# Recurrent scores as 64x64 chunk products, moved into the state update, with the second group's solve one step behind

## What is computed

```python
def _rwkv7_scan(r, w, k, v, kk, a):
    def step(state, inp):
        r_t, w_t, k_t, v_t, kk_t, a_t = inp
        sa = jnp.einsum('bhij,bhj->bhi', state, -kk_t)
        state = (state * w_t[:, :, None, :]
                 + sa[..., None] * (kk_t * a_t)[:, :, None, :]
                 + v_t[..., None] * k_t[:, :, None, :])
        y = jnp.einsum('bhij,bhj->bhi', state, r_t)
        return state, y
```

## Time and profile before

| | |
|---|---|
| median of 3 runs | 3903.39 us (3902.7 to 3903.99) |
| profiled execution | 3901.91 us, its span 3900.1 us |
| PE / PEld busy | 91% / 74% |
| DVE / ACT / POOL busy | 34% / 31% / 33% |
| mean granted TensorE clock | 0.943 |
| recurrent stage, four tiles | from 2056 to 2331 us of the span |

### The profile page before, as it was taken

How to read it: one execution, slowest core, us unless ns; L and a number is a source line. 1 busy time by engine, 2 the same in 40 slices (tenths; PEclk the granted TensorE clock), 3 DMA queues, 4 the chain that set the end, 5 groups by cost and what they waited for, 6 DMA issues and landing times. The chain is left out here.

```text
span 3900.1 us, 39057 instructions
## 1 busy us (share of the span) xinstructions
PE 3554.1 (91%) x16504; PEld 2867.9 (74%) x16504; DVE 1344.4 (34%) x1893; ACT 1213.1 (31%) x1795; POOL 1293.6 (33%) x531
## 2 busy tenths in 40 slices
PE   7868999999999999998977889999988989989987
PEld 6766778877677788875766767788876758767866
DVE  5963331232333312124463334201165143032432
ACT  4323332232443322334332112322243522242232
POOL 3423244443152444421420003344423404414432
PEclk9979999999999999989988889899989999999998
DMA  3212122222131222221220012222222202202231
GB/s 138 87 49 81 60 92 97 98 95 81 34 119 59 93 97 97 96 74 43 84 92 33 1 45 94 71 97 97 92 81 81 92 22 92 92 30 84 92 108 60
DMA packets 82807, 305.30 MB, mean 78 GB/s; under 512 B 8997, under 2 KB 10825, under 8 KB 81354
## 3 DMA queue, kind: packets, MB, share of 16 engines
q1 hardware_dynamic: 78368, 280.61, 21.3%
q10 hardware_dynamic: 4266, 22.21, 1.5%
HBM read 291.77 MB, written 11.02 MB: 78 GB/s over the span
## 5 line engine op out<-in xcount | busy, mean ns | idle before, releaser
L2569 POOL TENSOR_TENSOR WL<-RW,WH 128x1024 fp32r<-128x1024 f32 x527 | 1293.4, 2457 | 2574.1 <-ACT WH L261 2573.9
L266 PE MATMUL PS<-XH,WH 128*128 128x512 f32 x2968 | 1178.3, 397 | 100.3 <-POOL WL L2569 40.7
L267 PE MATMUL PS<-XL,WH 128*128 128x512 f32 x2968 | 1167.9, 394 | 0.0
L268 PE MATMUL PS<-XH,WL 128*128 128x512 f32 x2968 | 1166.8, 393 | 0.0
L261 ACT ACTIVATE WH<-RW 128x1024 fp32r<-128x1024 f32 x527 | 552.7, 1052 | 807.1 <-PE PS L268 661.3
L266 PEld LDWEIGHTS PS<-XH,WH 128*128 128x128 f32 x2968 | 565.2, 190 | 241.5 <-issue 57.5
L268 PEld LDWEIGHTS PS<-XH,WL 128*128 128x128 f32 x2968 | 564.9, 190 | 119.6
L267 PEld LDWEIGHTS PS<-XL,WH 128*128 128x128 f32 x2968 | 565.3, 190 | 117.8 <-issue 2.4
L266 PE MATMUL PS<-YH,WH 128*128 128x512 f32 (+1 forms) x928 | 351.9, 379 | 30.9 <-DVE YL L831 9.7
L267 PE MATMUL PS<-YL,WH 128*128 128x512 f32 (+1 forms) x928 | 350.1, 377 | 0.0
L268 PE MATMUL PS<-YH,WL 128*128 128x512 f32 (+1 forms) x928 | 349.9, 377 | 0.0
(11 more groups left out here) (449 smaller groups left out, 3363.3 us busy)
## 6 DMA issues: line engine op xcount, KB each, us to landing
RW<-in_units SPq DMA_DIRECT2D x527, 512.0 KB, 3.2
spill<-X ACTq DMA_DIRECT2D x2, 2048.0 KB, 7.7
X<-spill ACTq DMA_DIRECT2D x2, 2048.0 KB, 8.0
X<-in_xT SPq DMA_DIRECT2D x8, 256.0 KB, 7.1
A<-spill ACTq DMA_DIRECT2D x1, 2048.0 KB, 10.2
out_T<-X ACTq DMA_DIRECT2D x1, 2048.0 KB, 7.4
spill<-X ACTq DMA_DIRECT2D x1, 1536.0 KB, 5.1
spill_gates<-X ACTq DMA_DIRECT2D x1, 1536.0 KB, 6.1
```

Source lines behind the costliest of these rows:

```text
L266: mm(out, hi, xh, start=first, stop=False)
L267: mm(out, hi, xl, start=False, stop=False)
L268: return mm(out, lo, xh, start=False, stop=last)
L2569: nc.gpsimd.tensor_tensor(WL[:, u % SPLIT, :], RW[:, u % RAW, :], WH[:, u % SPLIT, :].bitcast(F32), ALU.subtract).then_inc(split_done, 1)
```

## The change

- The score products are cut by chunk. Instead of full 128-token products, each head makes two 64x64 results per matrix, one for each chunk, with 64 rows and 64 columns of the array: the off-diagonal chunk blocks are no longer computed. Six products per pair of heads become twelve, with 64, 128 and 128 columns in place of 128, 256 and 256. Their results lie in banks 4g to 4g + 3, so the groups no longer share banks.
- The masks are applied to the diagonal blocks alone: twelve instructions of 64 partitions x 256 elements in place of six of 128 x 512. The zeros elsewhere are written once at t = 0 by eight memsets (six of 128x512, one of 128x1024, one of 128x2048) that follow the wait for the DMAs. The wait for the previous tile's `y.mm` stands before the last four masks instead of before the first.
- The products `.w` become a function of their own, `weights_pe`.
- `scores_pe` of the next tile's group 0 is issued inside `state_pe`, between `u.mm` and `s.mm` of the first chunk; it waits for the previous `.at` of group 0. Group 1's scores come after the state and wait for `y` and `st`.
- The solve of group 0 starts after its own `.w`; `.w` and `.rhs` of group 1 come after group 0's step 0, and group 1's step s - 1 follows group 0's step s. Only the first application waits for `.rhs`.

```diff
-        scores = PS[:, 0:7:6, 0:256].rearrange("p w (j c) -> p w j c", j=2)
+        halves = [slice(0, 64), slice(64, P)]
         def scores_pe(st, t, g):
+            i, B = f"r{t}.{g}", 4 * g
+            if t:
+                st.wait(*([f"y{t - 1}", f"st{2 * t - 1}"] if g else [f"r{t - 1}.0.at"]))
+            for q in range(2):
+                j = 2 * g + q
+                for c in range(2):
+                    tok = slice(t * P + 64 * c, t * P + 64 * c + 64)
+                    for w, b in enumerate(halves):
+                        mm(PS[halves[c], B + w, q * 64:(q + 1) * 64], AR[j][b, t, 0, halves[c]], T(j)[b, tok], start=True, stop=True)
...
+            for q in range(2):
+                last = nc.tensor.transpose(PS[:, B + 2, 256 + q * P:256 + (q + 1) * P], AR[2 * g + q][:, t, 0, :], ident)
+            st.do(last, i + ".scores")
+        def weights_pe(st, t, g):
...
             st.wait(i + ".masked")
...
         def scores_dve(st, t, g):
+            if t == 0 and g == 0:
+                st.wait("ma.out1", "gb.out", "rk.out")
+                for x in (GS[0][0], GS[0][1], GS[0][2], GS[1][0], GS[1][1], GS[1][2]):
+                    st.do(v.memset(x, 0.0))
+                st.do(v.memset(RHS[:, :, P:2 * P], 0.0))
+                st.do(v.memset(RB, 0.0))
             st.wait(i + ".scores")
...
+            for c, r in enumerate(halves):
+                masked(q4(G2)[r, :, :, halves[c]], k[c][:, :, :, 0, :], "strictT", c)
+                masked(q4(G0)[r, :, :, halves[c]], a[c], "sub16", c)
+                masked(q4(G1)[r, :, :, halves[c]], b[c][:, :, :, 0, :], "sub16T", c)
+                masked(R4[r, :, :, P + 64 * c:P + 64 * c + 64], a[c], "off16", c)
+            if t:
                 st.wait_ge(*reached(f"y.mm{t - 1}"))
+            for c, r in enumerate(halves):
+                masked(RB0[r, :, :, halves[c]], b[c][:, :, :, 1, :], "chunkT", c)
+                masked(RB1[r, :, :, halves[c]], k[c][:, :, :, 1, :], "chunkT", c, i + ".masked")
...
             if step == 0:
                 product(0, lambda n: blk(G1, n), lambda n: blk(G0, n), ".d2")
                 product(1, lambda n: blk(G0, n), lambda n: blk(G1, n), ".d2t")
+                st.wait(i + ".rhs")
                 apply(G1, ".a1")
...
                 st.do(last, f"u.mm{n}")
+                if cc == 0 and t < TT - 1:
+                    scores_pe(st, t + 1, 0)
...
         def rw_pe(pe, st, e):
+            scores_pe(st, 0, 0)
             for t in range(TT):
-                scores_pe(st, t, 0)
                 scores_pe(st, t, 1)
-                st.wait_ge(*reached(f"r{t}.1.rhs"))
-                for step in range(STEPS):
-                    for g in range(2):
-                        solve_pe(st, t, g, step)
+                weights_pe(st, t, 0)
+                for step in range(STEPS + 1):
+                    if step < STEPS:
+                        solve_pe(st, t, 0, step)
+                    if step == 0:
+                        weights_pe(st, t, 1)
+                    else:
+                        solve_pe(st, t, 1, step - 1)
                 state_pe(st, t)
```

More of the change, by code:

```diff
@@ L1882, in program @@
         mq = lambda name: cst(name).rearrange("p (a b c) -> p a b c", a=1, b=1).to_broadcast([P, 2, 2, P])
-        scores = PS[:, 0:7:6, 0:256].rearrange("p w (j c) -> p w j c", j=2)
+        halves = [slice(0, 64), slice(64, P)]
         def scores_pe(st, t, g):
-            i = f"r{t}.{g}"
[L1887 to L1905, removed]
@@ new lines, in scores_pe @@
+            i, B = f"r{t}.{g}", 4 * g
+            if t:
+                st.wait(*([f"y{t - 1}", f"st{2 * t - 1}"] if g else [f"r{t - 1}.0.at"]))
+            st.wait_ge(*reached("p1.turned11"))
+            for q in range(2):
[4 more added lines that the diff above has]
+                        mm(PS[halves[c], B + w, q * 64:(q + 1) * 64], AR[j][b, t, 0, halves[c]], T(j)[b, tok], start=True, stop=True)
+                for c in range(2):
+                    tok = slice(t * P + 64 * c, t * P + 64 * c + 64)
+                    for w, b in enumerate(halves):
+                        o = PS[halves[c], B + w, 128 + q * P:128 + (q + 1) * P].rearrange("p (v c) -> p v c", v=2)
+                        mm(o, T(j)[b, tok], AR[j][b, t, :, halves[c]], start=True, stop=True)
+                for c in range(2):
+                    tok = slice(t * P + 64 * c, t * P + 64 * c + 64)
+                    for w, b in enumerate(halves):
+                        o = PS[halves[c], B + 2 + w, q * P:(q + 1) * P].rearrange("p (v c) -> p v c", v=2)
+                        mm(o, T(30 + j)[b, tok], AR[j][b, t, :, halves[c]], start=True, stop=True)
@@ L1906, in scores_pe @@
+            for q in range(2):
+                last = nc.tensor.transpose(PS[:, B + 2, 256 + q * P:256 + (q + 1) * P], AR[2 * g + q][:, t, 0, :], ident)
+            st.do(last, i + ".scores")
+        def weights_pe(st, t, g):
+            i = f"r{t}.{g}"
             st.wait(i + ".masked")
-            for n, h in enumerate(heads):
+            for n, h in enumerate(heads_of(g)):
                 j, b = h // 2, 64 * (h % 2)
-                last = mm(PS[:, 5, n * 64:(n + 1) * 64], blk(G2, n), T(8 + j)[:, t * P + b:t * P + b + 64], start=True, stop=True)
+                last = mm(PS[:, 4 * g + 3, 256 + n * 64:256 + (n + 1) * 64], blk(GS[g][2], n), T(8 + j)[:, t * P + b:t * P + b + 64], start=True, stop=True)
@@ L1910, in scores_pe @@
             st.do(last, i + ".w")
         def scores_act(st, t, g):
-            i = f"r{t}.{g}"
+            i, B = f"r{t}.{g}", 4 * g
             R4 = quad(RHS, g)
             st.wait(i + ".masked", i + ".w")
-            st.do(a_.activation(R4[:, :, :, 0:64], PS[:, 5, 256:512].rearrange("p (j w c) -> p w j c", j=2, w=2), ACT.Copy))
-            st.do(a_.activation(R4[:, :, :, 64:P], q4(PS[:, 5, 0:256]), ACT.Copy), i + ".rhs")
+            if t:
+                st.wait(f"u{2 * t - 1}")
+            st.do(a_.activation(R4[:, :, :, 0:64], PS[:, B + 2, 256:512].rearrange("p (j w c) -> p w j c", j=2, w=2), ACT.Copy))
@@ L1920, in scores_dve @@
+            st.do(a_.activation(R4[:, :, :, 64:P], q4(PS[:, B + 3, 256:512]), ACT.Copy), i + ".rhs")
         def scores_dve(st, t, g):
-            i = f"r{t}.{g}"
+            i, B = f"r{t}.{g}", 4 * g
             G0, G1, G2, G3 = GS[g]
-            st.wait(i + ".scores")
-            if g == 0 and t:
-                st.wait_ge(*reached(f"y.mm{t - 1}"))
[L1926 to L1936, removed]
+            if t == 0 and g == 0:
[4 more added lines that the diff above has]
+                st.do(v.memset(RB, 0.0))
@@ new lines, in scores_dve, with masked @@
+            st.wait(i + ".scores")
+            st.settle()
+            R4, RB0, RB1 = quad(RHS, g), quad(RB[:, :, 0, :], g), quad(RB[:, :, 1, :], g)
+            def masked(out, x, name, c, done=None):
+                m = cst(name)[halves[c], halves[c]].rearrange("p (a b c) -> p a b c", a=1, b=1).to_broadcast([64, 2, 2, 64])
+                st.do(v.tensor_tensor(out, x, m, ALU.mult), done)
+            a = [PS[r, B:B + 2, 0:P].rearrange("p w (q c) -> p w q c", q=2) for r in halves]
+            b = [PS[r, B:B + 2, P:3 * P].rearrange("p w (q v c) -> p w q v c", q=2, v=2) for r in halves]
@@ new lines, in scores_dve @@
+            k = [PS[r, B + 2:B + 4, 0:2 * P].rearrange("p w (q v c) -> p w q v c", q=2, v=2) for r in halves]
+            for c, r in enumerate(halves):
[3 more added lines that the diff above has]
+                masked(R4[r, :, :, P + 64 * c:P + 64 * c + 64], a[c], "off16", c)
+            if t:
+                st.wait_ge(*reached(f"y.mm{t - 1}"))
@@ L2099, in rw_act @@
                 scores_act(st, t, 0)
[L2100 to L2103, removed]
+                for step in range(STEPS + 1):
+                    if step < STEPS:
+                        solve_act(st, t, 0, step)
+                    if step == 0:
+                        scores_act(st, t, 1)
+                    else:
+                        solve_act(st, t, 1, step - 1)
                 if t == TT - 1:
@@ L2115, in rw_dve @@
                 scores_dve(st, t, 1)
-                for step in range(STEPS):
-                    for g in range(2):
-                        solve_dve(st, t, g, step)
+                for step in range(STEPS + 1):
+                    if step < STEPS:
+                        solve_dve(st, t, 0, step)
+                    if step:
+                        solve_dve(st, t, 1, step - 1)
                 state_dve(st, t)
```

## The result

The changed kernel takes 3845.4 us (3845.0 to 3848.2) against 3903.2; the ratio is 0.985 (95% interval 0.984 to 0.987). That is 57.8 us less where 51.2 were forecast, inside the range. The profiled execution has a span of 3843.2 us, 56.9 less than before.

A forecast was written before the change was run, and what follows sets the result against it. PE's single chain in the four recurrent tiles was taken as the bound, idle before each solve. Transitions 53.0, less 4.2 for scores in the state, plus 2.4 in tile 0: 51.2 us off, 3852.2; range 3837 to 3865.

The forecast's parts named there:

- Scores of group 1: After the output copy: 48 instructions 29 ns apart, 1.4 us, plus change-over 0.33 and transposes 0.44, ending at R + 2.85.
- R: Bookmark: start of a tile's output copy, 2126.77 in tile 0 before the change.
- The two-quarter rival: Array quarters run only in pairs: 0.75 us more for six groups of scores on the path, 3856.7; chance 0.15.
- Masks: DVE's twelve half-size masks per group start 0.33 us apart, 4.1 us (5.0 at 0.42); group 1's end at R + 7.0.
- Solve: Step 0 to U: 32.5 us at full clock, plus 1.2 for the skew and 1.0 for group 1's `.w`, 34.7.
- U: Bookmark: start of a tile's first state product, 2182.34 in tile 1 before the change; forecast at R + 38.5.
- The transitions: Three stretches from R to the next U: 17.1 us shorter in tile 1, 17.95 in tiles 2 and 3, 53.0 together.
- Scores inside the state update: First product needing DVE's addition comes 2.9 us after U instead of 1.47: 1.4 us later, three times, 4.2 lost.
- Tile 0: Memsets delay the masks by 6.5 us, yet the solve starts at 2075.8 instead of 2080.89: 2.4 us won, bounds 1.4 to 4.
- S: Bookmark: DVE's first instruction after the spill has landed, 2063.10 before; forecast the same.
- The clock in the state update: Low granted clock over state and outputs, 3.4 us lost per tile; change left at nought, 13.6 us if it never fell.
- The rival of a clock that never falls: The clock never falls in the recurrent stage: 3838.6 us; chance 0.13.

The follow-up runs named there:

- the run of halves in turn: Changed kernel with the same 64x64 score products, but one column half of the array finished before the other; 3854.9 us.
- the run without it: Changed kernel without the skew: group 1's `.w` stays behind group 0's step 0, then the groups go in step; 3844.4 us.
- the quarters in the old order: Changed kernel's 64x64 score products, twelve masks and memsets, with the three walks of the kernel before; 3906.2 us, ratio to before 1.001.
- the run with scores in both chunks: Changed kernel with group 0's scores divided: first pair of heads in chunk 0 of the state update, second pair and transposes in chunk 1; 3845.5 us.
- the scores after the state update: Changed kernel with group 0's scores of the next tile issued after the state update instead of inside it; 3872.6 us.
- memsets-ahead kernel: Changed kernel with six memsets ahead of the spill wait, the 128x2048 one cut and put behind group 1's masks; 3845.9 us, executions in two pairs.

## Why the prediction was right, point by point

- **Scores of group 1.** Forecast to end at R + 2.85, they ended at R + 2.36, where group 1's masks start (R + 2.39). The bound was the wrong one: I took 29 ns per instruction from rows of two quarters at work, but eight instructions of 64 columns start within 0.12 us (15 ns each) and eight of 128 columns within 0.22 (27 ns), 1.1 us for 48. The two-quarter rival falls with the run of halves in turn. The change-over to 128-row tiles was overpriced too: 0.33 us is the idle time of PEld there. From start to start it costs 0.10 us in the kernel before, where the last group takes 0.53 us until the transposes (2129.79) and the one ahead of it 0.43, and 0.11 in the changed one (0.33 after 2126.60 where it is 0.22 otherwise):

```profile
2128.83 0.60 PE L1900 MATMUL PS<-A 64*128 64x256 f32 x4
...
2129.26 0.60 PE L1902 MATMUL PS<-A 64*128 64x256 f32 x4
```

- **Masks.** 0.37 us apart, between the 0.33 that I took and the 0.42 that I bounded with; they ended at R + 6.85 where R + 7.0 was forecast. They start earlier and last longer, and PE comes earlier too, so the slack that I saw, 0.3 us, was a wait of 0.15.
- **Solve.** Step 0 to U was forecast at 34.7 us and took 35.4; the solve started 0.77 us sooner than forecast, so that U came at R + 38.46 against R + 38.5. That agreement to 0.1 us is luck: two errors of 0.7 us cancel. The late stalls were 0.88, 0.42 and 0.78 us of idle time where I had 1.05, 0.6 and 0.95 from start to start, and the skew was priced at 1.2 us where the run without it gives 1.6. These 0.4 us, and 0.3 by which group 1's `.w` starts later than the application ahead of it lets it (2131.93 instead of 2129.88 + 1.73), make up the 0.7. The transitions gave 52.8 us against 53.0.
- **Scores inside the state update.** Forecast 1.4 us a tile, found 0.8: the first product that needs DVE's addition starts 2.26 us after U (2117.09 in tile 0) against 1.47. In three tiles 2.4 us are lost instead of 4.2. From the first score to the transposes pass 1.31 us where I took 1.73, and from there to the next product 0.37 where I took 0.77: the quarters and the change-overs, as above. Against that, 0.17 us are added by the first products that need no addition (L2073), which now stand behind the scores.
- **Tile 0.** 2.7 us won against 2.4 forecast; the memsets took 6.5 us as worked out. But S itself came 2.7 us later, 0.74 of them before the stage and most of the rest in the landing of the spill, 7.9 us after its issue instead of 6.1; the prediction had left S as it was, without a reason:

```profile
spill_gates<-X ACTq DMA_DIRECT2D x1, 1536.0 KB, 6.1
```
```profile
spill_gates<-X ACTq DMA_DIRECT2D x1, 1536.0 KB, 7.9
```

This comes with the new order and is not scatter. In all twelve traces of kernels that make both groups' scores before the first masks, the landing takes 7.8 to 8.0 us; in the two with the old order (the kernel before, and the quarters in the old order) 6.1 and 6.0. In the same twelve, and not in the two, an instruction load (queue q8) moves between 2040 and 2070 us; in the changed kernel it falls between 2058 and 2062, beside the spill. That it delays the spill is argued from this alone, no run removes it.
- **The clock in the state update.** This is the term that was most wrong. I put it at nought, and it gave 6.5 us: U to R is 4.2 us shorter in sum although the scores add 2.4. The rival of a clock that never falls had part of the mechanism: two state updates of four stayed at 1.00 and one at 0.85. Its price was too high as well. 3.4 us per tile counts the waits for DVE as if they took double time at half clock; a tile that stayed at 1.00 took 10.2 us with 0.8 of scores in it where it was 12.0, so the low clock had cost some 2.6. What I argued against it, that the second chunk still works in bursts, agrees with the run with scores in both chunks: only with that wait filled too does it stay up each time. That the time lay inside the range, and near the forecast, owes something to errors that cancel: 6.5 us of clock and 1.8 of scores on one side, 2.7 of S on the other.
- **Sum.** Starting from 51.2 us: 1.8 more from the scores' place, 6.5 from the clock, nothing from tile 0 and transitions together (0.3 more and 0.2 less), 2.7 less by S: 56.9 in the profiled execution.

That it is the order that brings the gain, and not the smaller products, is shown by the quarters in the old order (3906.2 us); the scores after the state update (3872.6) show one half of that order's worth.

## What to carry to other kernels

Where a chain of small steps leaves TensorE idle, look for independent work of the next iteration to put into its waits, and read the clock of the stretch behind them: here the scores' place was worth some 8 us in waits and 19 in clock. Before speeding up a product, look at who evacuates it; splitting the products into quarters won nothing until the order changed, but by the layout in the code it made the results small enough for both groups to have banks of their own, which allowed the order. An edit that wins some microseconds by its own stage's trace can show nothing in the total, since the clock of later stages differs by more than that from kernel to kernel and, to judge by the two pairs of times above, from execution to execution; compare the stage, and then the total of an edit large enough. And what stands ahead of the stage can move with the order too, as the spill did.

## What was not expected of the hardware

- Four 64x64 quarters of the array work at once on fp32 data: eight instructions of 128 columns in 0.22 us with the quarters alternating, four in the same time when one column half goes first.
- The same work behind the last R took from 1568.6 to 1576.3 us in the traces; the first 25 us of it ran at a granted clock of 0.75 in the memsets-ahead kernel and 0.86 in the changed one. The two longest were kernels whose last R lay at 2270.63 and 2266.65; one at 2261.45 took 1569.0 and one at 2271.92 took 1568.6, so that the moment of the last R alone does not order them.
- Instructions of VectorE on 64 partitions and 256 elements start 0.37 us apart on average where those of 128 partitions and 512 elements start 0.60 apart: a quarter of the elements takes six tenths of the time, and as the pieces number twelve instead of six, they cost 4.46 us against 3.7.
- The spill of 1536 KB landed 7.8 to 8.0 us after its issue in the twelve traces with an instruction load between 2040 and 2070 us, and 6.0 and 6.1 us after it in the two without.
